# The mLSTM gate rows computed before the low-rank products, and two PSUM banks opened earlier in the first layer

## What is computed

```python
def mlstm_mixer(p, conv_prev, C0, n0, m0, conv_w, conv_b, ig_b, fg_b, norm_g):
    ...
    ig = p[..., 3 * W:3 * W + H] + ig_b
    lf = jax.nn.log_sigmoid(p[..., 3 * W + H:3 * W + 2 * H] + fg_b)
    h, C, n, m = mlstm_chunked(q, k, v, ig, lf, C0, n0, m0)
```

## Time and profile before

| | |
|---|---|
| three executions | 2192.77, 2197.46, 2201.22 us (median 2197.46) |
| the profiled execution | 2191.85 us |
| its span, first to last instruction | 2189.7 us |
| mean granted TensorE clock | 0.979 of full speed |

### The profile page before, as it was taken

The page is one execution under the profiler, slowest core; times in us unless marked ns, Lnnn a source line. Parts: engine busy times, 40 slices in busy tenths (PEclk is TensorE's granted clock), DMA queues, the critical chain, the costliest instruction groups (busy, mean ns, idle before and its releaser), DMA issues.

```text
span 2189.7 us, 38223 instructions
## 1 busy us (share of the span) xinstructions
PE 2017.9 (92%) x13140; PEld 1234.5 (56%) x13140; DVE 1424.4 (65%) x3431; ACT 858.9 (39%) x2484; POOL 748.9 (34%) x658
## 2 busy tenths in 40 slices
PE   7999979999999888999899898899999997889997
PEld 6777768874444223555478776788644442234444
DVE  2425454589999998544442355645899889975545
ACT  2221222044545775433331213221554557853333
POOL 0400000025555776554312000000355557755552
PEclk9999989999999999999999998999999999999999
DMA  7330233579999999999843202436699999999995
GB/s 281 116 117 2 81 107 135 186 262 326 325 354 378 373 348 357 364 378 395 335 188 116 98 5 78 146 134 252 232 331 354 370 375 360 370 383 391 369 384 234
DMA packets 121547, 568.77 MB, mean 260 GB/s; under 512 B 42504, under 2 KB 44712, under 8 KB 61864
## 3 DMA queue, kind: packets, MB, share of 16 engines
q0 software_dynamic: 76032, 389.07, 47.1%
q1 hardware_dynamic: 43648, 174.07, 21.8%
q10 hardware_dynamic: 1696, 3.45, 0.4%
HBM read 724.58 MB, written 6.58 MB: 334 GB/s over the span
## 4 chain that ended last, share of the span: by engine, by line
PE 59%; DVE 21%; issue 9%; DMA 5%; ACT 4%; POOL 1%; another core or an unknown queue 1%; DVEq 0%; SPq 0%; ACTq 0%; POOLq 0%
PE ps L1018 12%; PE ps L1099 12%; PE ps L609 10%; PE ps L674 7%; DVE arena L2107 5%; PE ps L1047 3%; DMA ring<-in_uv,arena 3%; PE ps L931 3%; PE ps L945 3%; PE ps L970 2%; DVE arena L2132 1%; DMA arena<-in_uv,arena 1%; DVE arena L2000 1%; DVE arena L1991 1%; DVE arena L1990 1%
## 5 line engine op out<-in xcount | busy, mean ns | idle before, releaser
L1538 POOL DMA_INDIRECT arena<-in_uv,arena x264 | 337.4, 1278 | 269.5 <-PE ps L1018 221.9
L1538 POOL DMA_INDIRECT ring<-in_uv,arena x264 | 321.7, 1219 | 255.1 <-PE ps L1018 207.5
L2107 DVE SCALAR_TENSOR_TENSOR arena<-arena 128x1024 bf16<-128x1024 f32 x264 | 319.7, 1224 | 120.5 <-DMA arena<-in_uv,arena 113.7
L2107 DVE SCALAR_TENSOR_TENSOR arena<-ring,arena 128x1024 bf16<-128x1024 f32 x264 | 320.4, 1224 | 114.2 <-DMA ring<-in_uv,arena 108.0
L1018 PE MATMUL ps<-arena 64*64 64x512 f32 x2112 | 292.7, 626 | 43.7 <-ACT arena L1430 43.4
L1018 PE MATMUL ps<-ring,arena 64*64 64x512 f32 x2112 | 287.3, 616 | 37.6 <-ACT arena L1430 35.6
L1428 ACT ACTIVATE arena<-arena 128x1 f32<-128x1 f32 x528 | 105.8, 200 | 502.2 <-DVE arena L2107 501.2
L1528 POOL COPY arena<-arena 128x8 uint32 (+1 forms) x66 | 39.4, 598 | 729.3 <-DVEq L2074 728.9
L1099 PEld LDWEIGHTS ps<-hold,ub 128*128 128x128 f32 x1024 | 180.3, 190 | 160.0 <-issue 142.8
L1099 PE MATMUL ps<-hold,ub 128*128 128x256 f32 x1024 | 268.1, 397 | 0.0
L674 PE MATMUL ps<-xn,ring 128*128 128x264 f32 x1024 | 245.2, 398 | 14.1 <-remote 12.7
(11 more groups left out here) (452 smaller groups left out, 2436.7 us busy)
## 6 DMA issues: line engine op xcount, KB each, us to landing
ring<-in_w SPq DMA_DIRECT2D x84, 1024.0 KB, 5.0
ub<-in_uv SPq DMA_DIRECT2D x64, 512.0 KB, 7.8
ub<-in_ud SPq DMA_DIRECT2D x48, 512.0 KB, 7.5
hold<-in_ud SPq DMA_DIRECT2D x16, 512.0 KB, 6.0
ring<-in_uv,arena POOLq DMA_INDIRECT x264, 9.0
arena<-in_uv,arena POOLq DMA_INDIRECT x264
ub<-in_w SPq DMA_DIRECT2D x4, 1024.0 KB, 11.2
hold<-in_st SPq DMA_DIRECT2D x2, 2048.0 KB
```

Source lines behind the costliest of these rows:

```text
L1538: e.indirect_dma_start(out=row(k), out_offset=None, in_=A["uv"], in_offset=bass.IndirectOffsetOnAxis(ap=ix[:, par, k:k + 1], axis=0), **sk ...
L2107: stt(prod[:, n % 2, :], u, 1.0, xtok[:, tt, :], ALU.mult, ALU.mult, accum_out=hid[:, k:k + 1]).then_inc(S("dve_hid"), 1)
```

## The change

Three things are done. First, PE makes the gate rows (the former L866) ahead of the low-rank products, into bank 0, as soon as ACT has copied out the last column tile; ACT adds the biases between its Sigmoid and the low-rank results, into a new place if_rows, a piece of the tile hold that is not used until the end of the mixers; PE's head sums, which write bank 0 too, wait for these two activations; DVE reads rows 0 and 1 from the new place. Second, the counters' tuples follow the new order. Third, in the first layer ACT raises bank_free of banks 0 and 1 ahead of its first activation; in the second layer nothing of that changes.

```diff
-PE_STEPS = ("ket", "vt", "dl", "hy", "lr", "kk", "rk", "tr", "bv", "rot", "if", "rows", ...
+PE_STEPS = ("ket", "vt", "dl", "hy", "if", "lr", "kk", "rk", "tr", "bv", "rot", "rows", ...
-ACT_STEPS = (..., "proj", "lr", "kk", "e", "sv0", "vpad", "bv", "r0", "r2", ...
+ACT_STEPS = (..., "proj", "lr", "r0", "kk", "e", "sv0", "vpad", "bv", "r2", ...
...
+        if_rows = hold[:, 7456:7456 + 2 * N].rearrange("p (a b) -> p a b", b=N)
...
+                e.wait_ge(S("act_step"), step("act_proj"))
+                for kt in range(KT):
+                    m = mm(ps[0:36, 0, 0:N], w_if[:, kt, :], xn[:, kt, :], start=kt == 0, stop=kt == KT - 1)
+                m.then_inc(S("pe_step"), 1)
                 e.wait_ge(S("act_step"), step("act_lr"))
                 e.wait_ge(S("dve_hy"), 1)
...
                 e.wait_ge(S("dve_kk2"), 1)
+                e.wait_ge(S("act_step"), step("act_r0"))
                 for pr in range(PR):
                     m = mm(bank(pr), C("headsum"), t1[:, pr, :], start=True, stop=True)
...
                 causal(0, qr, kq, proj[:, RT + 4:RT + 6, :])
-                for kt in range(KT):
-                    m = mm(ps[0:36, 2, 0:N], w_if[:, kt, :], xn[:, kt, :], start=kt == 0, stop=kt == KT - 1)
-                m.then_inc(S("pe_step"), 1)
...
+            for b in range(2):
+                e.sem_inc(bank_free[b], 1)
             first_with_gain(0)
...
-                for b in range(2):
-                    e.sem_inc(bank_free[b], 1)
+                if l:
+                    for b in range(2):
+                        e.sem_inc(bank_free[b], 1)
                 root(2 * l + 1, rstd)
...
                 act(proj[:, RW + 7, :], proj[:, RW + 7, :], ACT.Sigmoid).then_inc(S("act_step"), 1)
+                e.wait_ge(S("pe_step"), step("pe_if"))
+                act(if_rows[0:4, 0, :], ps[0:4, 0, 0:N], ACT.Identity, bias=V("ig_b")[0:4, :])
+                act(if_rows[0:4, 1, :], ps[32:36, 0, 0:N], ACT.Identity, bias=V("fg_b")[0:4, :]).then_inc(S("act_step"), 1)
                 e.wait_ge(S("pe_step"), step("pe_lr"))
...
-                e.wait_ge(S("pe_step"), step("pe_if"))
-                act(rows[0:4, 0, :], ps[0:4, 2, 0:N], ACT.Identity, bias=V("ig_b")[0:4, :])
-                act(rows[0:4, 1, :], ps[32:36, 2, 0:N], ACT.Identity, bias=V("fg_b")[0:4, :]).then_inc(S("act_step"), 1)
-
                 e.wait_ge(S("dve_r1"), 1)
...
-                R = lambda n, lo=0, hi=N: rows[0:4, n, lo:hi]
+                R = lambda n, lo=0, hi=N: (if_rows if n < 2 else rows)[0:4, n, lo:hi]
```

More of the change, by code:

```diff
@@ L79 @@
 BIG = 3.0e38
-PE_STEPS = ("ket", "vt", "dl", "hy", "lr", "kk", "rk", "tr", "bv", "rot", "if", "rows", "svt", "sa", "po", "mean", "it0", "it1", "vd")
+PE_STEPS = ("ket", "vt", "dl", "hy", "if", "lr", "kk", "rk", "tr", "bv", "rot", "rows", "svt", "sa", "po", "mean", "it0", "it1", "vd")
 NORM_EPS, RWKV_EPS, HEAD_EPS = 1e-6, 64e-5, 1e-5
 HG, RW, RT, ML = 0, 8, 16, 24
-ACT_STEPS = ("hv", "hg", "ln", "eb", "ket", "vx", "proj", "lr", "kk", "e", "sv0", "vpad", "bv", "r0", "r2", "conv", "em", "dt", "sv", "svt", "og", "ysq", "it0", "it1")
+ACT_STEPS = ("hv", "hg", "ln", "eb", "ket", "vx", "proj", "lr", "r0", "kk", "e", "sv0", "vpad", "bv", "r2", "conv", "em", "dt", "sv", "svt", "og", "ysq", "it0", "it1")
 PAR = dict(mu=(0, 8), w0=(8, 2), a0=(10, 2), kk=(12, 2), ka=(14, 2), rk=(16, 2), ln_g=(18, 2), ln_b=(20, 2),
```

## The result

The changed kernel takes 2181.48 us (median of 5 executions, 2175.80 to 2182.80), the kernel before 2194.53 in its five; the ratio is 0.9931, interval 0.9905 to 0.9957. The forecast was -8.7 us with 0.74 for no difference that a measurement can tell. The time lies at the lower edge of the stated range, and the difference, 13 us by the medians and 15 by the ratio, is over the 11 us that count as faster. Measured twice more (e4, e10) the ratio is 0.9946 and 0.9946. Over all these executions the changed kernel's mean is 2184.0 us (24 executions). That of the kernel before, as it was timed beside it and beside e1 to e11, is 2197.0 (77; e1's own twelve left aside): 13.0 us more.

What follows compares the result with a forecast made beforehand. PE, on 59% of the chain that ends last, was taken as the bound; -3.0 - 0.6 + 0.1 - 2.6 - 2.6 = -8.7 us gave 2183.2 from the profiled 2191.85, or 2188.8 on the median's scale, range 2181 to 2196.

Steps and rivals of the forecast that it cites:

- start: First layer's first products: with banks opened early, PE starts at 11.8 instead of 14.82 us; -3.0 us.
- low-rank part: Behind the last column tile: gate rows fill PE's gap, low-rank products run at full clock; -0.6 and +0.1 us.
- old place: Behind the retention mixer: gate rows' 3.68 us leave PE, 1.1 become a new wait; -2.6 us in each layer.
- C: Rival at the first layer's start: the weights' landing, not the bank, held PE; only -5.7 us, 2191.8, chance 0.08.
- B: Rival: the clock takes a part, by slow low-rank products or a start worth 1.5; about 2192.6 us, chance 0.2.
- the 3.68 us, the hidden store and the semaphore behind it: Behind the retention mixer: sixteen gate-row products took 3.68 us, hiding ACT's 0.36 us store issue ahead of a bank semaphore.
- A: Rival: the old place gives all 3.7 us in each layer, bank free in time; -10.9 us, 2186.6, chance 0.13.
- D: Rival in the PEER part: gathers and large blocks collide worse, each wait 0.033 us longer; 2206.2 us, chance 0.05.
- only the 0.6 and the 0.1 pass on: After the low-rank part the chain runs through DVE; only -0.6 and +0.1 us carry further, PE's faster clock brings nothing.
- the 33.3 us that were to stay: From the spreading of the rows to the 7 us wait for the gate block: this span would be unchanged.

Runs made afterwards that it cites:

- e4: The changed kernel again, no edit; ratio to the kernel before 0.9946.
- e10: The changed kernel a third time, no edit; ratio to the kernel before 0.9946.
- e1: The kernel before again, no edit; ratio 0.9999, profiled execution 2193.20 us.
- e11: The changed kernel with the first layer's banks opened as before, so only the gate rows moved, timed once more; ratio to the kernel before 0.9938.
- e5: The kernel before with sixteen products, results unused, in PE's idle stretch behind the last column tile; ratio 0.998.
- e6: The changed kernel with the sixteen gate-row products made at the old place once more, results unused; ratio to the kernel before 0.9975.
- e7: The changed kernel with ACT raising the two bank semaphores ahead of issuing the store; ratio to the kernel before 0.9965.
- e2: The kernel before with only the first layer's two banks opened early; ratio 0.9969.
- e3: The changed kernel with the first layer's banks opened as before, so only the gate rows moved; ratio to the kernel before 0.9964.
- e16: The kernel before with its gap filled by sixteen unused products, as e5, profiled again; 2182.57 us, one time.
- e18: The kernel before with its gap filled by sixteen unused products, a further draw of e16; 2198.18 us, one time.
- e15: The kernel before, no edit, a further profile; 2199.21 us, one time.
- e12: The kernel before, no edit, one more profile; 2196.28 us, one time.
- e8: The changed kernel with semaphores raised ahead of the store and unused products of constants in PE's retention-mixer and gate-block waits; ratio to the kernel before 0.9948.

## Why the prediction was right or wrong

**Right in its terms.** Taken from stretches without the falls further on, the change's own parts are: start 20.7 to 18.0, -2.7 (forecast -3.0); low-rank part, first layer 162.7 to 162.4, -0.3 (forecast -0.6), second layer 159.6 to 159.2, -0.4 (forecast +0.1); old place 23.6 to 21.1 in each layer, -2.5 and -2.5 (forecast -2.6 each). The sum, before rounding, is -8.5, the forecast -8.7.

- *The banks of the first layer.* The mechanism was as stated, and C is out: PE started 0.06 us behind the first block's end (11.33 + 0.50). The 0.3 are not lost to ACT: PE starts 2.9 us earlier, and from there to the sum of squares it takes 6.1 us on average instead of 5.9, which is well within the 5.1 to 6.6 that this time ranges over. The Trainium skill (TensorE: Matmul & The Clock Gate, What's actually happening) lets the number of slow products differ between executions; the profiles agree, stretch (a) ran from 19.9 to 21.5 us with the old start.
- *The gate rows ahead of the low-rank products.* Start, duration and cover came out to 0.05 us, and 2.68 us at full clock was forecast as 2.7. The second layer's +0.1 was reckoned against a single profile in which its low-rank products ran half fast. e5 shows that the clock alone is the gain, and B, slow low-rank products or a start worth 1.5, did not come true.
- *The old place.* e6 and e7 confirm the 3.68 us, the hidden store and the semaphore behind it; A, the whole 3.7, did not come true: the stretches (e) show 2.5. The change came out near A's time for another reason.
- *D, the gathers,* did not come true: their waits are unchanged (114.1 against 113.7 us), and the span outside the mixers is 1.6 us longer on average, well inside its range.

**Wrong in what it left out.** The step that failed is the sentence that after the low-rank part "only the 0.6 and the 0.1 pass on", with "so PE's faster clock beyond 162 us brings nothing". The forecast priced a fall of the clock where the change touches PE and took every fall elsewhere as fixed, as one profile showed it. The runs show that falls further on come and go between executions of one kernel, each 1.3 to 3.2 us on the chain in (c) and (d), and that there are fewer of them in the changed kernel. With it the mixers take 12.7 us less: 8.5 by the terms and 4.2 beyond them. Of the 4.2, (c) and (d) make 2.8, and the stretch behind (e), up to the transposes of the samples' vectors, 1.3 (67.9 to 67.2 us per layer on average), which is also where the 33.3 us that were to stay became 32.0.

Three and six profiles are few, but the granted clock of every timed execution says the same. Within either kernel an execution whose mean granted clock is lower by 0.001 is 1.37 us longer (fitted over the 84 executions of the kernel before that list a clock beside e1 to e11, and over the 24 of the changed one). The mean clock is 0.9781 before and 0.9814 after. That difference goes with 4.5 of the 12.9 us between these executions and leaves 8.4, close to the 8.5 of the terms. (The old order's falls at the low-rank products are part of the difference of the clocks, while their 0.3 and 0.4 us are in the 8.5 already, so the two agree to about a microsecond and not better.)

**What makes the falls rarer** is open. Each edit alone moved the time by more than its own stretches: the start 6.8 us instead of 2.7 (e2), the rows 7.9 and 13.6 instead of 5.8 (e3, e11), the filled gap 4.4 instead of 0.7 (e5). The whole change has 11.9 to 15.2 instead of 8.5, so these surpluses don't add up. That the filled gap causes the rarer falls of the second layer rests on 5 of 7 against 2 of 11, which speaks for it and does not prove it; the 3.3 us of e5 and e16 to e18 are no proof either. In the first layer (d) has a fall in 1 of 6 profiles with the early start (e2, e4, e6, e7, e10, after) and in 8 of 12 with the late one, but chance alone gives a split as uneven in about one case of eight, and the rows name something that goes with these falls far better. It is how long PE takes from its very first product to the sum of squares, that is (a) less PE's start, which is 14.7 to 14.9 us with the late start and 11.7 to 12.0 with the early one. In the ten profiles that have a fall in the first layer's (c) it takes 5.1 to 5.9 us, in the ten that have none 6.0 to 6.6, whichever the kernel and whichever the start. Two executions of the kernel before, e15 with falls in (c) and (d) and e12 with none:

```profile
14.81 6.06 PE L609 MATMUL ps<-arena,ub 128*128 128x264 f32 x16 [14.81 <-ACTq L422]
20.71 3.72 PE L582 MATMUL ps<-xn,const 128*128 128x264 f32 x16
```

```profile
14.84 6.57 PE L609 MATMUL ps<-arena,ub 128*128 128x264 f32 x16 [14.84 <-ACTq L422]
21.24 3.72 PE L582 MATMUL ps<-xn,const 128*128 128x264 f32 x16
```

So whether PE's clock falls in the first layer, from about 170 us later on, goes with how long this first part took. That an earlier start as such changes anything there is not shown. For the second layer the rows at hand name no such sign.

**The range and the chances.** The range's lower end took in a better low-rank part and the scatter of executions (2184.5 less half of 8.4 is 2180.3, which the forecast rounds to 2181), and held the time by 0.5 us. The chance of 0.74 for no difference was too sure: the forecast lay 2.3 us from the 11 that divide, and single executions scatter by some 20 us (2186.19 to 2207.05 in 33 of the kernel before, 2175.36 to 2193.91 in 24 of the changed one). The three executions shown before the forecast had scattered by only 8.4.

## What to carry to other kernels

Work that PE must do anyway is worth most in a gap after which the clock would have fallen: it is taken off its old place, and the products behind the gap run at full clock. Falls later on may become rarer too, which can be worth as much as a term of the sum. Before an instruction is taken from where it stands, look at what it hid there; here a store's issue ahead of two semaphores took 1.1 of 3.7 us back. And one profile is one draw: where the granted clock dips on the chain, take several profiles and compare stretch by stretch, and don't fill waits on a part that another engine ends, since the gap only moves to where it costs (e8).

## What was not expected of the hardware

The clock's falls differ between executions of the very same program: the retention mixer's stretch took 14.2 to 14.3 us at a granted clock of 1.00 or 16.6 to 17.4 us at 0.73 to 0.84, with the same number of products, and in no profile anything between. PE is busy there for 9.9 of 14.2 us. The clock stayed at 1.00 through the sixteen products with only 36 columns of weights and the low-rank products behind them (the rows of 155 to 159 us of the changed kernel; the same in e5).
